# A hybrid decoder step: the sample tokens' high and low parts as 64 stationary columns, and loads of v and of the state at other places

## The chip, the cores and the metric

The kernel runs on one core of one Trainium2 chip. The metric is the device time of one execution in microseconds (us): 1620.35 us as the median of three runs, which lie between 1619.05 and 1621.43.

## The reference

One layer of a decoder, for a prompt of 1024 tokens and for 32 sample tokens (8 sequences of 4), model width 1024, everything in float32. Cut to what matters:

```python
z = x @ w_in                      # 1024 -> 4176 columns
mq, mk, mv, mo, mi, mf, aq, ak, av, iq, ik, iw = split(z)
q, k, qi, ki = partial_rope(aq), partial_rope(ak), partial_rope(iq), partial_rope(ik)
h_m, (C, n, m) = mlstm(mq, mk, mv, mo, mi, mf, C0, n0, m0)   # 4 heads of 128
idx = top_k(sum_h(iw * relu(qi @ ki)), 256)                  # the sample tokens: 65
h_a = softmax(q @ k[idx]) @ v[idx]                           # 8 heads of 64
x = layer_norm(ALPHA * x + concat(h_m, h_a) @ w_out)
y = layer_norm(ALPHA * x + (silu(x @ w_gate) * (x @ w_up)) @ w_down)
```

Outputs are y, the keys, values and indexer keys of all tokens, and the mLSTM state (C, n, m) after the prompt and after the samples. The sample tokens read their past keys and values from paged caches, and begin with a state (state_C and others) of their own.

## The kernel before, in words

**Tiles.** The tokens are nine tiles: eight of 128 prompt tokens, and a ninth (`LAST`) of the 32 sample tokens. A float32 product is made of three products of rounded parts: each operand is split into a high part (one rounding copy, on ACT) and a low part (the difference, on DVE or POOL), and PE adds high·high, high·low and low·high (`PARTS`) over 8 blocks of 128 rows (`KD`): 24 matmuls for each tile and each slice of weights.

**Projections.** The list `jobs` sets the order of the first stage on all engines. A job is one PSUM bank of a ring of six (`RING`): PE fills it and ACT or DVE empties it. Ten token-major units (iq, av, ak, aq, mv, two slices of 256 columns each, kind "tm") have the tokens as the stationary operand (L2209): 24 matmuls of 256 columns per tile, nine tiles per unit. ACT copies the bank into a row of `stage` (L2329), POOL rotates it where rope is due (`rope_tile`, L2406 to L2410), SP stores it to DRAM (`store`, L2106). After the ninth tile of most units POOL makes the low part of the weight slice two units ahead (`low`, L2418), which PE needs to begin that unit, and which needs ACT's high part (L2283). Jobs of kind "tr" (L2226) turn the rotated tiles, "scd" (L2259 on PE, copied on ACT at L2375) makes the indexer scores of the samples. Then come feature-major units mk, mq, mo (kind "fm", L2266), which ACT copies (L2382) and SP stores (L2161).

Beside this DVE selects the top-k (L2484 to L2564): it begins when the samples' scores are in SBUF, and steps through bisection passes (L2514) and the resolution of ties (L2542 to L2553). Behind it, in DVE's program, come the rows of the forget gate (`dve_rows`, b_row at L922), and ACT waits for them (`act_forget`, L959) in the middle of its copies of the "fm" jobs.

**Later stages.** Sparse attention of the prompt (`pe_attention`; L373 turns weights, L408 multiplies by v, which `sp_attention` loads at L563 from the stored output), attention of the samples (`pe_samples`, semaphore `smp_values` counts its two halves, PE L670), the mLSTM (`pe_mlstm`, nine steps n; the sample sequences use the buffer `cn`, filled from state_C, and the sample values `mvs`, both loaded in `sp_mlstm` at L892 and L894), the output product (`pe_product`, L1543, two halves h of 512 columns over nine tiles, added to x by DVE at L1613), then the FFN and the last normalisation.

**What sets the order at the mLSTM.** SP issues the loads of the prompt's and samples' values (`mv_and_one`, L620 and L623) behind the samples' cache loads, then the loads of L892 and L894, and then that of mo (L896). `pool_mlstm` waits for both halves of the samples' values and sets constants to one (L1277 to L1279). `act_columns` copies the samples' values (L1001). In step n of `act_mlstm` ACT first makes weights and keys of step n+1 (L1218, L1234), then takes the outputs of step n (`take_outputs`, L1251: four copies that are scaled by the inverse denominator of L1392), and in the later steps also makes high parts of the out weights (L1578).

## Time and profile before

| | us |
|---|---|
| median of three runs | 1620.35 |
| profiled execution: its own time | 1620.41 |
| its span on the core | 1618.6 |
| PE busy | 1566.2 (97%) |
| DVE busy | 763.0 (47%) |
| ACT busy | 449.1 (28%) |
| POOL busy | 401.9 (25%) |
| projections, about | 0 to 492 |
| prompt attention | 492 to 624 |
| samples | 625 to 654 |
| mLSTM | 656 to 730 |
| output product | 726 to 833 |
| FFN and end | 833 to 1618.6 |

The profile is of one execution, which took 0.06 us more than the median of the runs. Its span is the time between the first and the last instruction on the core, and the 1.8 us by which the execution's own time is longer lie around it. Busy time is the time in which an engine has an instruction at work; shares are of the span. The mean granted clock of PE is 0.991 of full speed.

### The profile page before, as it was taken

To read this page: it belongs to the slowest core of one execution; us is meant where nothing else is said; L and a number is where in the kernel's file an instruction comes from. 1 tells how busy PE (TensorE), PEld (TensorE's weight loads), DVE (VectorE), ACT (ScalarE), POOL (GpSimd) and SP (SyncE) were. 2 spreads that over 40 slices of the span, in tenths; PEclk is the share of its full clock that TensorE was granted. 3 is DMA by queue.
4 is the path that set the end of the run, shared out by engine and by line. 5 is a ranking of instruction groups with operands and counts; after the bars stand their busy time and mean duration, and the time that the engine had idled before them with its cause. 6 is when DMAs were issued, how large, how long until landed. Compare 5 with 4: busy or idle time off the path is not lost.

```text
span 1618.6 us, 27247 instructions
## 1 busy us (share of the span) xinstructions
PE 1566.2 (97%) x10677; PEld 1448.6 (89%) x10677; DVE 763.0 (47%) x1655; ACT 449.1 (28%) x929; POOL 401.9 (25%) x386
## 2 busy tenths in 40 slices
PE   7999999999998998689999999999999999999998
PEld 7986799999996766588789999999999999999986
DVE  2008599999834664454554413233131322413146
ACT  4336423222134564263252111211212021121100
POOL 3620155222110001425394122212221221122200
PEclk9999999999999999899999999999999999999999
DMA  5210231122216003624202111111101111111012
GB/s 183 71 43 18 64 103 49 58 85 79 80 68 253 28 21 95 182 86 160 79 1 79 53 53 53 28 53 53 53 27 53 53 49 31 53 53 53 1 53 82
DMA packets 117596, 110.65 MB, mean 68 GB/s; under 512 B 16186, under 2 KB 102206, under 8 KB 117474
## 3 DMA queue, kind: packets, MB, share of 16 engines
q1 hardware_dynamic: 117474, 108.90, 21.6%
q8 instruction: 92, 1.51, 0.4%
q14 instruction: 30, 0.25, 0.1%
HBM read 88.82 MB, written 19.95 MB: 67 GB/s over the span
## 4 chain that ended last, share of the span: by engine, by line
PE 55%; issue 0%; DVE 0%; DVEq 0%
PE bank L1765 31%; PE bank L1743 13%; PE bank L1543 6%; PE bank L1930 3%; PE bank L1925 0%; PE bank L1683 0%; PE bank L1128 0%; PE bank L1142 0%; PE bank L1145 0%; PE bank L1157 0%; DVE y_tm L1966 0%; DVE y_tm L1958 0%; DVE stats L1949 0%; DVEq L64 0%; DVE state L1353 0%
## 5 line engine op out<-in xcount | busy, mean ns | idle before, releaser
L1765 PE MATMUL bank<-x_split,gate_up_split 128*128 128x352 f32 x3168 | 510.9, 323 | 2.4 <-issue 2.4
L1765 PEld LDWEIGHTS bank<-x_split,gate_up_split 128*128 128x128 f32 x3168 | 507.5, 188 | 3.3 <-issue 3.3
L2209 PE MATMUL bank<-w_split,xT_split 128*128 128x256 f32 (+1 forms) x2160 | 271.9, 283 | 3.1 <-ACT w_split L2281 1.8
L2209 PEld LDWEIGHTS bank<-w_split,xT_split 128*128 128x128 f32 (+1 forms) x2160 | 256.8, 179 | 9.5 <-ACT kT L2365 2.9
L1848 DVE TENSOR_TENSOR hidden<-silu,bank 128x352 f32<-128x352 f32 x66 | 34.4, 522 | 411.5 <-ACT silu L1810 411.4
L1743 PE MATMUL bank<-hidden_split,weight_split 128*128 128x352 f32 x1296 | 209.2, 322 | 0.0
L1743 PEld LDWEIGHTS bank<-hidden_split,weight_split 128*128 128x128 f32 x1296 | 208.0, 188 | 0.0
L1884 POOL TENSOR_TENSOR gate_up_split<-gate_up,gate_up_split 128x2048 fp32r<-128x2048 f32 x22 | 104.3, 4741 | 376.7 <-ACT gate_up_split L1802 376.7
L2514 DVE TENSOR_SCALAR_CACHE_REDUCE chosen<-scores,level 128x384 uint8<-128x384 f32 (+2 forms) x198 | 174.3, 943 | 1.2
L1751 DVE TENSOR_TENSOR y_acc<-y_acc,bank 128x352 f32<-128x352 f32 x216 | 112.6, 521 | 84.5 <-PE bank L1743 83.3
L2266 PE MATMUL bank<-xT_split,w_split 128*128 128x352 f32 x864 | 138.8, 323 | 1.2 <-ACT feature_stage L2382 1.2
L2266 PEld LDWEIGHTS bank<-xT_split,w_split 128*128 128x128 f32 x864 | 138.3, 188 | 1.5 <-ACT feature_stage L2382 1.5
L1810 ACT ACTIVATE silu<-bank 128x352 f32<-128x352 f32 x66 | 30.7, 466 | 365.5 <-PE bank L1765 365.4
L2418 POOL TENSOR_TENSOR w_split<-w_unit,w_split 128x2048 fp32r<-128x2048 f32 (+1 forms) x16 | 73.5, 4593 | 196.7 <-ACT w_split L2283 196.7
L1543 PE MATMUL bank<-out_weight_split,x_split 128*128 128x512 f32 (+1 forms) x384 | 91.3, 396 | 0.0
L2329 ACT ACTIVATE stage<-bank 128x256 f32<-128x256 f32 (+1 forms) x90 | 34.6, 384 | 190.0 <-PE bank L2209 182.6
L1543 PEld LDWEIGHTS bank<-out_weight_split,x_split 128*128 128x128 f32 (+1 forms) x384 | 67.9, 178 | 20.4
L1888 POOL TENSOR_TENSOR weight_split<-down_weight,weight_split 128x2048 fp32r<-128x2048 f32 x10 | 46.0, 4597 | 159.5 <-ACT weight_split L1816 159.5
L1816 ACT ACTIVATE weight_split<-down_weight 128x2048 fp32r<-128x2048 f32 x10 | 19.2, 1916 | 186.6 <-PE bank L1743 186.6
L520 ACT ACTIVATE attention_weights<-attention_weights,row_minima 128x1024 f32<-128x1024 f32 (+7 forms) x64 | 49.2, 770 | 46.7 <-DVE row_minima L451 46.6
L451 DVE CUSTOM_DVE_ANT_0 attention_weights<-bank,scores 128x512 f32<-128x512 f32 (+1 forms) x48 | 30.1, 667 | 63.6 <-PE bank L362 63.6
L1802 ACT ACTIVATE gate_up_split<-gate_up 128x2048 fp32r<-128x2048 f32 x22 | 42.1, 1916 | 22.6 <-DMA gate_up<-in_w_up_dram 22.5
(293 smaller groups left out, 1641.3 us busy)
## 6 DMA issues: line engine op xcount, KB each, us to landing
w_unit<-in_w_in_dram SPq DMA_DIRECT2D x16, 1024.0 KB, 5.6
gate_up<-in_w_gate_dram SPq DMA_DIRECT2D x22, 512.0 KB, 4.0
gate_up<-in_w_up_dram SPq DMA_DIRECT2D x22, 512.0 KB, 5.3
down_weight<-in_w_down_dram SPq DMA_DIRECT2D x11, 1024.0 KB, 5.2
scratch_dram<-feature_stage SPq DMA_DIRECT2D x36, 176.0 KB, 1.8
scores<-in_x_prompt_dram SPq DMA_DIRECT2D x8, 512.0 KB, 4.9
out_dram<-stage SPq DMA_DIRECT2D x32, 128.0 KB, 1.7
out_weight<-in_w_out_dram SPq DMA_DIRECT2D x16, 256.0 KB, 6.9
```

The lines of the kernel that those rows point to most:

```text
L520: act.activation(x, x, ACT.Exp, bias=lows[:, n % 4, e, chunks[n] - 1:chunks[n]], scale=-1.0, accum_out=rowsum[:, o % 2, 2 * p + e:2 * p + ...
L1543: mm = pe.matmul(product_bank(m)[0:r, :], mix(i, a)[:, k, 0:r], wo[h][:, k, b, :], start=(k == 0 and (a, b) == PARTS[0]), stop=(k == KD - ...
L1743: mm = pe.matmul(PS[6 + n % 2][:, 0:cols.stop - cols.start], wds[:, a, k, d * P:(d + 1) * P], hs[:, 2 * s + k, b, cols], start=(k == 0 and ...
L1751: dve.tensor_tensor(y, y, PS[6 + n % 2][:, 0:cols.stop - cols.start], ALU.add).then_inc(d_added, 1)
L1765: mm = pe.matmul(PS[2 * c + w][:, 0:CH], gs[u][:, a, w, k, :], xs[:, b, k, c * CH:(c + 1) * CH], start=(k == 0 and (a, b) == PARTS[0]), st ...
L1884: pool.tensor_tensor(gs[u][:, 1], graw, gs[u][:, 0].bitcast(F32), ALU.subtract).then_inc(g_lo, 1)
L1888: pool.tensor_tensor(w[:, 1], wdraw, w[:, 0].bitcast(F32), ALU.subtract).then_inc(wd_lo, 1)
L1930: mm = pe.matmul(bank, hs[:, 2 * s + k, a, tile_cols(i)], w[:, b, k, 512 * half:512 * half + 512], start=False, stop=(s == 0 and k == 1 an ...
L2209: mm = pe.matmul(bank[0:rows(i), 0:HALF], xs1[:, a, k, tile_cols(i)], w[:, b, k, :], start=((k, a, b) == terms[0]), stop=((k, a, b) == ter ...
L2266: mm = pe.matmul(bank[:, 0:CH], wsplit[n_unit % 2][:, a, k, (m % 2) * P:(m % 2 + 1) * P], xs1[:, b, k, c * CH:(c + 1) * CH], start=(k == 0 ...
L2418: pool.tensor_tensor(lo, wraw[n >= 4][:, k], hi.bitcast(F32), ALU.subtract).then_inc(w_lo, 1)
L2514: dve.tensor_scalar(chosen[i], score[i], level_f[:, n:n + 1], 0.0, op, ALU.add, accum_out=count[:, n:n + 1]).then_inc(topk_step, 1)
```

## The change

**Sample tile.** The split of the samples' x is also written with the high and the low part side by side, as 64 stationary columns per block, for blocks 0 to 6; block 7 stays as it was. A "tm" job of the tile LAST multiplies these 64 columns by the high and by the low slice of the weights (two matmuls per block) and block 7 in three: 17 matmuls where 24 were. Rows 0 to 31 of the bank hold the high parts' sums, rows 32 to 63 those of the low parts (with low·low, which was left out before). ACT makes two copies in place of one, and POOL adds the two halves (`sum_halves`, semaphore `sample_summed`). ACT's copy of a tile LAST waits for the sum before it, its copy of "scd" for the fourth sum, and its first "fm" copy for all ten. `pe_product` does the same for its tile LAST, where DVE adds the second half with one more instruction. ACT and DVE split the samples' x (and the mixed heads) with some more instructions.

**Waits and loads.** SP's wait for all feature stores moves from the end of its first program to a place behind the nine loads of v. The loads of `cn` and `mvs` move from SP to POOL's queue, ahead of the constants of `pool_mlstm`, with a wait for the first half of the samples' values only, and for the stores of the two mv units. For steps n over 4 one DVE multiplication behind the reciprocal takes the place of ACT's four copies in `take_outputs`.

```diff
@@ sp_attention / sp_mlstm / end of SP's first program
                 sp.dma_start(v_tm[0:r, i, :], src).then_inc(v_loaded, 16)
 
+            for s in range(FST):
+                sp.wait_ge(fstored[s], 16 * (len(fm_no) // FST))
             sp_mlstm_loads(sp)
...
-            sp.wait_ge(smp_values, 1)
-            for h in range(MH):
-                sp.dma_start(mvs[SMP * h:SMP * h + SMP, 0:P], mv_dram[SEQ:T, P * h:P * h + P]).then_inc(c_in, 16)
-            for h in range(MH):
-                sp.dma_start(cn[:, h, :, 0:P], state_C[0, :, h].rearrange("b d e -> d b e")).then_inc(c_in, 16)
...
-            for s in range(FST):
-                sp.wait_ge(fstored[s], 16 * (len(fm_no) // FST))
             sp_rest(sp)
@@ act_mlstm, pool_mlstm, dve_mlstm
-                take_outputs(n)
+                if n <= MH:
+                    take_outputs(n)
...
             pool_rows_low(pool)
+            pool.wait_ge(smp_values, 1)
+            for h in range(MH):
+                pool.dma_start(cn[:, h, :, 0:P], state_C[0, :, h].rearrange("b d e -> d b e")).then_inc(c_in, 16)
+            for u in range(2):
+                s = stage_no["tm", "mv", u, LAST] % STG
+                pool.wait_ge(stored[s], 16 * seen[s])
+            for h in range(MH):
+                pool.dma_start(mvs[SMP * h:SMP * h + SMP, 0:P], mv_dram[SEQ:T, P * h:P * h + P]).then_inc(c_in, 16)
             pool.wait_ge(att_values, N2)
...
+                if n > MH:
+                    dve.wait_ge(den_done, n + 1)
+                    dve.wait_ge(h_ps, n - 1)
+                    o = o_banks[:, :, 0:2 * VE].rearrange("p b (i n) -> p b i n", n=VE)[:, :, :, 0:P]
+                    dve.tensor_tensor(htm[:, n % 2].rearrange("p (b i) n -> p b i n", b=2), o,
+                                      inv.unsqueeze(3).to_broadcast([P, 2, 2, P]), ALU.mult).then_inc(o_taken, 2)
@@ pe_product and its addition
+                if i == LAST and k < KD - 1:
+                    for b in range(2):
+                        mm = pe.matmul(product_bank(m)[0:2 * SMP, :], split_mix(k), wo[h][:, k, b, :],
+                                       start=(k == 0 and b == 0), stop=(k == 6 and b == 1))
...
+                if i == LAST:
+                    total.then_inc(sample_summed, 1)
+                    dve.wait_ge(sample_summed, len(sample_no) + h + 1)
+                    total = dve.tensor_tensor(x, product_bank(m)[r:2 * r, :], x, ALU.add)
@@ projections: PE, ACT, POOL
-                        terms = [(k, a, b) for k in range(KD) for a, b in PARTS]
+                        ks = list(range(KD)) if i < LAST else [0, 1, 2, 3, 4, 5, 7, 6]
+                        terms = [(k, a, b) for k in ks for a, b in PARTS if i < LAST or a == 0 or k == KD - 1]
...
+                            out, tokens = bank[0:rows(i), 0:HALF], xs1[:, a, k, tile_cols(i)]
+                            if i == LAST and k < KD - 1:
+                                out, tokens = bank[0:2 * SMP, 0:HALF], split_sample(k)
+                            mm = pe.matmul(out, tokens, w[:, b, k, :],
...
+                        if sample_no[job]:
+                            act.wait_ge(sample_summed, sample_no[job])
+                        act.activation(st[0:SMP, :], bank[0:SMP, 0:HALF], ACT.Copy)
+                        out = act.activation(low_of(job), bank[SMP:2 * SMP, 0:HALF], ACT.Copy)
...
                 elif kind == "scd":
+                    act.wait_ge(sample_summed, 4)
...
+            def sum_halves(job):
+
+                pool.wait_ge(freed, pos[job] + 1)
+                both = stage[0:SMP, stage_no[job] % STG, :]
+                pool.tensor_tensor(both, both, low_of(job), ALU.add).then_inc(sample_summed, 1)
...
                 if job == ("tm", "ik", 0, LAST):
+                    sum_halves(("tm", "av", 0, LAST))
...
                     low(4)
+                    sum_halves(("tm", "av", 1, LAST))
...
             for n in range(unit_no["aq", 1] + 3, len(units)):
+                if units[n - 2][0] == "mv":
+                    sum_halves(("tm",) + units[n - 2] + (LAST,))
                 low(n)
```

What the order of instructions shows of this, at three places (line numbers behind the change are those of the changed file, where L2280 is the old L2209, L2297 the old L2226, L2509 the old L2418, L2479 the new sum and L2497 to L2501 the old rope lines).

PE, the end of the second unit (iq1): its eighth and ninth tile, with the turns of the tiles before between them. Before:

```order
L2209 MATMUL bank<-w_split_73,xT_split 128x256 x24
L2226 MATMUL bank<-square,stage 128x128 x2
L2209 MATMUL bank<-w_split_73,xT_split 32x256 x24
L2226 MATMUL bank<-square,stage 128x128 x2
L2216 MATMUL bank<-xT_split,w_small_split 80x352 x24
L2226 MATMUL bank<-square,stage 128x128 x2
```

and now:

```order
L2280 MATMUL bank<-w_split_73,xT_split 128x256 x24
L2297 MATMUL bank<-square,stage 128x128 x2
L2280 MATMUL bank<-w_split_73,sample_x_split_81 64x256 x8
L2280 MATMUL bank<-w_split_73,sample_x_split_82 64x256 x4
L2280 MATMUL bank<-w_split_73,xT_split 32x256 x3
L2280 MATMUL bank<-w_split_73,sample_x_split_83 64x256 x2
L2297 MATMUL bank<-square,stage 128x128 x2
```

The ninth tile has 14 matmuls of 64 stationary columns and 3 of 32 in place of 24 of 32; the rest stands as it did.

POOL, from the last rope of the indexer's keys to the first of ak. Before (`w_split_72` is here the low part of weight slice 4, the first of ak):

```order
L2408 TENSOR_TENSOR rope_products<-stage,rope 32x2x8
L2410 TENSOR_TENSOR stage<-rope_products 32x2x16
L2435 TENSOR_SCALAR sample_index_select<-small,sample_index_weights 128x32 x2
L2418 TENSOR_TENSOR w_split_72<-w_unit_75,w_split_72 128x2048
L2406 TENSOR_TENSOR rope_products<-stage,rope 128x4x16
L2407 TENSOR_TENSOR rope_products<-stage,rope 128x4x8
L2408 TENSOR_TENSOR rope_products<-stage,rope 128x4x8
L2410 TENSOR_TENSOR stage<-rope_products 128x4x16
```

and now:

```order
L2501 TENSOR_TENSOR stage<-rope_products 32x2x16
L2479 TENSOR_TENSOR stage<-stage,sample_scores 32x256
L2527 TENSOR_SCALAR sample_index_select<-small,sample_index_weights 128x32 x2
L2509 TENSOR_TENSOR w_split_72<-w_unit_75,w_split_72 128x2048
L2479 TENSOR_TENSOR stage<-stage,sample_scores 32x256
L2497 TENSOR_TENSOR rope_products<-stage,rope 128x4x16
L2498 TENSOR_TENSOR rope_products<-stage,rope 128x4x8
L2499 TENSOR_TENSOR rope_products<-stage,rope 128x4x8
L2501 TENSOR_TENSOR stage<-rope_products 128x4x16
```

The sum of unit av0 stands ahead of `wsel` (L2435, now L2527), and that of av1 behind the low part of slice 4; `sample_scores` is the buffer that holds the low half of the sum until the samples' scores are written into it.

POOL, the beginning of its part of the mLSTM. Before:

```order
L996 TENSOR_TENSOR rows_low<-b_row,rows_high 4x1056
L996 TENSOR_TENSOR rows_low<-gates,rows_high 4x1056
L1277 MEMSET mv_and_one 128x32
L1278 MEMSET mv_by_head 128x1
L1279 MEMSET mq_by_sample 128x1152
L1284 TENSOR_TENSOR mv_by_sample_104<-mv_split,own_sample 96x8x128
L1284 TENSOR_TENSOR mv_by_sample_113<-mv_split,own_sample 96x8x128
```

and now:

```order
L1018 TENSOR_TENSOR rows_low<-b_row,rows_high 4x1056
L1018 TENSOR_TENSOR rows_low<-gates,rows_high 4x1056
L1300 DMA c_and_n_sample<-in_state_C_dram 128x8x128 x4
L1305 DMA mv_by_head<-scratch_dram 32x128 x4
L1308 MEMSET mv_and_one 128x32
L1309 MEMSET mv_by_head 128x1
L1310 MEMSET mq_by_sample 128x1152
L1315 TENSOR_TENSOR mv_by_sample_108<-mv_split,own_sample 96x8x128
```

Eight DMA issues stand now between the low parts of the rows and the three constants, and the same eight are gone from SP's queue, where they stood between the loads of `mv_and_one` and that of mo.

## Rows read from the trace of the kernel before

**Rows 1.** PE's waits by releaser, whole span (total us, times, longest us)

```profile
PE bank L1072 <- DMA c_and_n_sample<-in_state_C_dram: 3.8, 1, 3.8
PE bank L408 <- DMA v<-out_dram: 3.1, 1, 3.1
PE bank L1128 <- DVE state L1353: 2.6, 1, 2.6
...
PE bank L2266 <- ACT feature_stage L2382: 1.2, 1, 1.2
...
PE bank L2226 <- POOL stage L2410: 0.9, 2, 0.7
```

**Rows 2.** Timeline of PE, two neighbouring tiles of one unit (start, busy us)

```profile
69.55 3.08 PE L2209 MATMUL bank<-w_split,xT_split 128*128 128x256 f32 x24
...
72.60 3.06 PE L2209 MATMUL bank<-w_split,xT_split 128*32 128x256 f32 x24
```

**Rows 3.** Timeline of PE, the output product's last tile

```profile
827.03 5.79 PE L1543 MATMUL bank<-out_weight_split,x_split 128*32 128x512 f32 x24
```

**Rows 4.** Timeline of DVE, start of the top-k chain

```profile
190.14 0.18 DVE L2484 TENSOR_TENSOR sample_scores<-sample_scores,small 32x32 f32<-32x32 f32 x1 [13.97 <-ACT sample_scores L2375]
```

**Rows 5.** Timeline of POOL, low part of weight slice 4

```profile
185.34 4.57 POOL L2418 TENSOR_TENSOR w_split<-w_unit,w_split 128x2048 fp32r<-128x2048 f32 x1 [59.45 <-ACT w_split L2283]
```

**Rows 6.** Groups of POOL by line, with shapes kept apart

```profile
L1660 POOL TENSOR_TENSOR x_split<-y_acc,x_split 128x512 fp32r<-128x512 f32 x16 | 20.7, 1293 | 12.1 <-DVE x_split L1637 12.1
```

**Rows 7.** Timeline of ACT, the forget-gate rows

```profile
441.59 1.09 ACT L959 ACTIVATE m_row<-b_row 4x1056 f32<-4x1056 f32 x1 [17.96 <-DVE b_row L922]
```

**Rows 8.** Timeline of DVE, top-k's last steps

```profile
418.87 1.02 DVE L2546 SCALAR_TENSOR_TENSOR running<-running,count,equal 128x768 f32<-128x768 f32 x1
...
424.23 5.30 DVE L2546 SCALAR_TENSOR_TENSOR running<-running,count,equal 128x896 f32<-128x896 f32 x1
```

**Rows 9.** Timeline of POOL, low part of weight slice 14

```profile
423.70 4.88 POOL L2418 TENSOR_TENSOR w_split<-w_unit,w_split 128x2048 fp32r<-128x2048 f32 x1 [18.42 <-ACT w_split L2283]
```

**Rows 10.** Busy time by windows, after attention's wait (PEclk is the granted clock)

```profile
505.50:508.00 2.50, 2.50 (x32) 2.20 (x32) 0.00 (x0) 0.60 (x2) 0.00 (x0) 0.73 1.03 412
508.00:511.00 3.00, 3.00 (x20) 2.81 (x18) 1.38 (x2) 0.42 (x1) 0.00 (x0) 0.65 1.02 407
```

**Rows 11.** Timeline of SP's queue, end of the projections

```profile
492.49 0.32 SPq L2161 DMA_DIRECT2D scratch_dram<-feature_stage  x1
496.48 4.13 SPq L563 DMA_DIRECT2D v<-out_dram  x9
```

**Rows 12.** Timeline of PE, two late mLSTM steps

```profile
707.06 1.06 PE L1128 MATMUL bank<-mv_and_one,mk_weighted 128*128 128x129 f32 x8
...
711.51 1.06 PE L1128 MATMUL bank<-mv_and_one,mk_weighted 128*128 128x129 f32 x8
```

**Rows 13.** Timeline of ACT, the take of steps 6, 7 and 8

```profile
710.85 1.15 ACT L1251 ACTIVATE hidden_by_token<-bank,denominator 128x128 f32<-128x128 f32 x4 [1.16 <-DVE denominator L1392]
...
716.58 1.15 ACT L1251 ACTIVATE hidden_by_token<-bank,denominator 128x128 f32<-128x128 f32 x4 [1.16 <-DVE denominator L1392]
...
723.35 1.15 ACT L1251 ACTIVATE hidden_by_token<-bank,denominator 128x128 f32<-128x128 f32 x4 [1.16 <-DVE denominator L1392]
```

**Rows 14.** Timeline of DVE, a multiplication of the same size

```profile
723.17 0.66 DVE L1399 TENSOR_TENSOR mixT<-bank,iqT 128x512 f32<-128x512 f32 x1
```

**Rows 15.** Timeline of PE, samples' values of the first half

```profile
646.46 1.12 PE L670 MATMUL bank<-v,sample_weights_turned 32*128 32x512 f32 x2
```

**Rows 16.** Timeline of SP's queue, the state loads

```profile
655.19 7.84 SPq L894 DMA_DIRECT2D c_and_n_sample<-in_state_C_dram  x4
```

**Rows 17.** Timeline of ACT, the first use of the mLSTM sample values

```profile
656.04 0.63 ACT L1001 ACTIVATE mv_split<-mv_and_one 96x512 fp32r<-96x512 f32 x1 [3.09 <-DMA mv_and_one<-scratch_dram]
```

**Rows 18.** Timeline of POOL, the first constant of the mLSTM stage

```profile
652.44 0.15 POOL L1277 MEMSET mv_and_one<- 128x32 f32 x1 [20.77 <-PE bank L670]
```

**Rows 19.** Busy time by windows, the values' loads

```profile
650.00:655.00 5.00, 3.45 (x26) 1.36 (x19) 1.11 (x6) 0.60 (x1) 1.16 (x3) 1.00 1.08 251
```

More of the change, by code:

```diff
@@ L1532, in pe_product @@
         def pe_product(pe, h, i, between=None):
-            r, m = rows(i), h * TILES + i
+            m = h * TILES + i
             if m >= 3:
                 pe.wait_ge(added, m - 2)
-            for k in range(KD):
+            order_k = list(range(KD)) if i < LAST else [0, 1, 2, 3, 4, 5, 7, 6]
+            for k in order_k:
                 if i == 0:
@@ L1570, in mix_low @@
                 eng.wait_ge(mix_hi, 2 * i + j + 1)
-                eng.tensor_tensor(mix(i, 1)[:, k, :], mixT[:, k, tile_cols(i)], mix(i, 0)[:, k, :].bitcast(F32), ALU.subtract)\
-                    .then_inc(done, 1)
+                whole = [[(mix(i, part)[:, k, :], mixT[:, k, tile_cols(i)])] for part in range(2)]
+                for (hi, src), (lo, _) in zip(*(whole if i < LAST else [sample_mix(j, 0), sample_mix(j, 1)])):
+                    low = eng.tensor_tensor(lo, src, hi.bitcast(F32), ALU.subtract)
+                low.then_inc(done, 1)
         def out_high(act, h, j):
@@ L2319, in _ @@
                                          bank[:, :].rearrange("p (k n) -> p k n", k=4)[:, :, 0:rows(i)], ACT.Copy)
+                    for dst, src in sample_parts(j, bank, 0) if i == LAST else ():
+                        out = act.activation(dst, src, ACT.Copy)
                 elif kind == "tm":
@@ L2378, in _ @@
                     f = fm_no[job]
+                    if f == 0:
+                        act.wait_ge(sample_summed, len(sample_no))
                     if f >= FST:
```

71 lines of the change are left out of this document (58 added, 13 removed).

## Prediction

> **What bounds the kernel now.** I first read PE's waits, because PE works through nearly all of the span: the reader should see that the whole list is small, and that four entries lie where the change reaches, 3.8 us for the samples' state, 3.1 for v, 2.6 for the mLSTM state and 1.2 for ACT's feature copy, and that POOL has held PE up by 0.9 us in the first units [rows 1]. Then the timelines of PE at a sample tile, to price the matmuls. Then, because time that PE saves is only kept if nothing else sets the end of its stage, I followed ACT's longest wait in the projections back: 17.96 us until DVE's b_row, ended at 441.59 us [rows 7]. DVE works through its top-k from 190.14 us [rows 4] to there almost without a pause. So the end of the projections hangs on DVE, and PE, which runs six banks ahead, feels only 1.2 us of that wait [rows 1].
>
> A result under 0.2% (3.2 us) from 1620.35 cannot be told from no change.
>
> **A. The sample tile in the projections.** A tile with 32 stationary columns is busy for 3.06 us, one with 128 for 3.08 [rows 2]: what a matmul costs does not hang on these columns, so 64 cost the same, and one is 3.06/24 = 0.128 us. Seven fewer in each of ten units are worth 10 x 0.89 = 8.9 us of PE. I expect to collect almost none of it.
> - The first unit (iq0) loses its 0.89 to the wait for POOL (0.9 us in all) [rows 1], which hangs on the weights' loads and splits and not on PE.
> - iq1 and av0 bring everything 1.8 us forward. DVE's chain starts with the copy of the samples' scores, and that copy now waits for av1's sum, which stands on POOL behind the low part of slice 4. This part runs from 185.34 for 4.57 us [rows 5], thus ends at 189.91; moved forward by 1.8, and with the sum behind it, it ends at 188.1 + 0.65 = 188.8. The sum's 0.65 is half of the 1.29 us that POOL takes for 512 columns [rows 6]; were it 1.29, 189.4. With an estimated 0.5 us for the copy and its hand-over, DVE starts at about 189.3 in place of 190.14, 0.8 us sooner (0.2 to 0.8); av1's own 0.89 is hidden behind POOL.
> - Near its end DVE's L2546 on 896 columns took 5.30 us, where 768 columns took 1.02 [rows 8]; it started at 424.23, while POOL worked on slice 14 from 423.70 to 428.58 [rows 9], and ended with it. By the neighbour it would have taken 1.2, so 4.1 were lost. Slice 14 now comes some seven units x 0.89 = 6.2 to 7 us earlier, at about 417, and there meets the L2546 on 768 columns (418.87 before, some 418.1 now), which would then be held until 421.5: a new block of 3.4 in place of the 4.1. Between blocks of 2.6 and 4.6 us I take a gain of 0.7.
> - So DVE ends about 1.5 us sooner (0.2 to 2.3), and with it ACT's wait; PE reaches that point 7 us sooner and stands idle for about 6.7 us in place of 1.2. What follows so long a pause may run at a lower clock: after the pause of 3.1 us in attention the granted clock was 0.73 for 2.5 us and 0.65 for 3.0 [rows 10], which is 2.5 x 0.27 + 3.0 x 0.35 = 1.7 us lost. After the 1.2 us I see none. I take 1.7 (0 to 3).
>
> A is then -1.5 + 1.7, near zero: **+0.2** (-2.3 to +2.8).
>
> **B. The output product.** The row of 24 matmuls for the sample tile is busy for 5.79 us, 0.241 each [rows 3]; 14 fewer over two halves are **-3.4** us, on the path, since PE goes from this tile straight to the FFN. The second DVE addition (about 0.66 as [rows 14]) and the three more operations on the samples' mixed heads lie beside other tiles' matmuls; PE waits for POOL's and ACT's last tile only later, so I let between 2 and 3.4 through.
>
> **C. The load of v.** SP issues the last feature store at 492.49 (0.32 us long) and v only at 496.48, when its stores have landed [rows 11]: that is the 3.7 us that go. The nine issues take 4.13, PE's wait ends at 505.5, some 4.9 us after the last of them. Issued from 492.8 on, v lands at about 501.9, before PE is ready at 502.4. The 3.1 us go [rows 1], and with them the pause and the 1.7 us at a lower clock [rows 10]: **-4.8** (-2.7 if the clock falls all the same and the landing lags). What is late next is only the loads behind the moved wait, which the mLSTM needs 150 us later.
>
> **D. ACT's take.** PE's own step is 4.45 us (707.06 to 711.51) [rows 12]. ACT's takes lie 5.73 and 6.77 us apart at the end [rows 13]: take, high parts of the out weights, weights and keys fill ACT, and PE waits 2.6 us for what hangs on them [rows 1]. Without the take (1.15) ACT has no wait for the denominator in its chain either, and PE sets the step: (5.73 - 4.45) + (6.77 - 4.45) = 3.6 us. The last take falls from 1.15 to some 0.66, the time of a DVE multiplication of 128x512 [rows 14]: 0.5. DVE then has some 3.7 us of work in a 4.45 us step. **-4.1** (-2 to -4.3).
>
> **E. State and sample values.** PE waits 3.8 us, to 668.7, for the state [rows 1], which SP issues from 655.19 for 7.84 us, 1.96 each [rows 16], behind the values' loads. POOL may issue it once the first half of the samples' values is there, after PE's L670 of 646.46 [rows 15], at about 647.7. Had it nothing beside it, it would land 7 us sooner, and all 3.8 go. But from 650 to 655 the DMA engines are full (share 1.08) with the values' loads [rows 19], for which ACT waited 3.09 us until 656.04 [rows 17], and which start the stage. With half of the engines' time from 647.7 on, these loads would need up to 8.4 us more, as long as they still ran before. So E lies between -3.8 and -3.8 + 8.4 = +4.6. If POOL issues at SP's pace, the state's loads come in one by one and take less than half: I put the delay at 2.4, nearer the free end, **-1.4**. POOL's price of an issue is in no row; its constants, at 652.44 before [rows 18], are needed at about 656.
>
> The Trainium skill, in "DMA: Bandwidth & Descriptors", section "SWDGE vs HWDGE vs iDMA", says that a DMA issued from GpSimd has its descriptors computed by software, with a slower setup than one from SP, and that the two feed different queues between which each DMA engine goes round-robin. No row of this trace shows a load from POOL. By that page's fit (section "Anatomy of one DMA — SWDGE (gpsimd) path") 512 KB would take an estimated 3.2 us, which by itself would land the state in time and make the sum 1604.5; by its round-robin the values lose half, which is the second rival below.
>
> **Sum.** 0.2 - 3.4 - 4.8 - 4.1 - 1.4 = -13.5 against the profiled execution's 1620.41, which is 0.06 over the median: **1607** us.
>
> **The rivals.**
> 1. *The saved matmuls are kept.* If ACT's wait ended with PE (DVE ending over 7 us sooner), A would be -8.0 (nine units) and no clock lost: 1598.7. Against it: the 17.96 us [rows 7]. For it: 4.1 us of DVE's chain are a collision that could miss altogether [rows 8, 9]. Chance 0.12.
> 2. *State against values.* The DMA engines share evenly, E is +4.6 and the rest holds: 1613. For it: the full engines [rows 19] and ACT's wait [rows 17]; against: 7.84 us of spread issues [rows 16]. Chance 0.22.
> 3. *The pause costs more clock.* Over 3 us behind the pause of 6.7, as it is twice as long as the one in [rows 10]; A is +3: 1610. Chance 0.12.
> 4. *POOL's issues gate the mLSTM.* The constants stand behind eight issues. At SP's 1.96 us each [rows 16] they would end at 647.7 + 15.7 + 1.3 = 664.7, 8.6 late; with the state's wait gone E would be +4.8, still a gain in all (1613.2). The change becomes slower than before by 0.2% when E passes +15.3, that is when the constants are 19 us late, at 3.3 us for an issue. Then some 1624. For it: these are other issues than any in the trace, and 512-byte rows; against: four of the eight are loads of only 16 KB. Chance 0.03.
>
> **How the numbers follow.** Forecast 0.51, the rivals 0.12, 0.22, 0.12 and 0.03. The range goes from rival 1 to rival 2 with the bounds of E and D, leaving out the better part of rival 1 and of rival 4: 1600 to 1614. Faster by over 0.2%: all but rival 4 and the case that it meets rival 3, 0.94; same 0.03; slower 0.03.
>
> **What would show it.** Right: PE's list of waits without v, the state and the mLSTM state, and with 6 to 7 us at L2266 for ACT's feature copy; ACT's L959 ending at about 440; a granted clock under 1 just behind it, and 1.0 at 505; late mLSTM steps of 4.45 us; sample tiles of 17 matmuls in 2.2 us. Wrong: ACT's copy of the samples' values later than 660, POOL's constants later than 656, a DVE chain that ends where it did (then A is a loss), or PE passing the feature copies without a longer pause than before.

## The result and the profile after

The changed kernel takes 1630.28 us (median of four runs, 1629.57 to 1631.72) against 1620.89 us of the kernel before (1619.05 to 1621.54): the ratio is 1.0066, with a 95% interval of 1.005 to 1.0082. It is 9.4 us slower; 1607 had been forecast, with 1600 to 1614 as the range.

The page of the profiled execution (1630.6 us) shows at once that the matmuls did go: PE is busy for 10.4 us less than before (1566.2), and the span is 10.2 us longer (1618.6).

```profile
span 1628.8 us, 27102 instructions
...
PE 1555.8 (96%) x10593; PEld 1442.3 (89%) x10593; DVE 773.0 (47%) x1664; ACT 448.4 (28%) x927; POOL 415.2 (25%) x405
...
q0 software_dynamic: 704, 2.16, 0.5%
...
L1832 PE MATMUL bank<-x_split,gate_up_split 128*128 128x352 f32 x3168 | 515.3, 324 | 10.2 <-issue 7.8
```

The last line is the FFN's first group, which idled for 2.4 us in the kernel before and idles for 10.2 now. PE's waits by releaser (total us, times, longest us), to be held against [rows 1]:

```profile
PE bank L2337 <- ACT feature_stage L2463: 12.9, 1, 12.9
PE bank L1063 <- ACT c_and_n_sample L1031: 8.9, 1, 8.9
PE bank L1832 <- issue: 7.8, 4, 2.5
...
PE bank L1832 <- DVE hidden L1915: 2.4, 2, 1.3
```

The waits for v, for the state and for the mLSTM state are gone, as forecast. In their place stand 12.9 us for ACT's feature copies (1.2 before, 6.7 forecast), 8.9 us for a copy of ACT's at the mLSTM that was hardly waited for before, and 10.2 us in the FFN, of which the prediction said nothing.

The starts of the same PE instructions in the two timelines give the loss stage by stage (us):

| PE reaches | before | after | lead of before | change in the stage |
|---|---|---|---|---|
| the end of the pause at the feature copies | 445.56 | 451.42 | 5.86 | +5.86 |
| the first multiplication by v (L408) | 505.50 | 510.32 | 4.82 | -1.04 |
| the end of the samples' attention (L1022) | 654.51 | 657.80 | 3.29 | -1.53 |
| the mLSTM's spreads (L1041) | 657.18 | 669.00 | 11.82 | +8.53 |
| the samples' outputs (L1072) | 668.66 | 677.00 | 8.34 | -3.48 |
| a late mLSTM step (L1128) | 702.61 | 707.16 | 4.55 | -3.79 |
| the out product (L1543) | 726.29 | 727.53 | 1.24 | -3.31 |
| the FFN (L1765) | 833.45 | 831.43 | -2.02 | -3.26 |
| the end | 1618.6 | 1628.8 | 10.2 | +12.22 |

**The FFN** is the largest loss, though the change touches nothing in it. Its two groups of weights run in a loop, and PE jumps back three times. PE's timeline at the first jump, after:

```profile
1009.79 8.43 PE L1832 MATMUL bank<-x_split,gate_up_split 128*128 128x352 f32 x52
1019.47 0.74 PE L1832 MATMUL bank<-x_split,gate_up_split 128*128 128x352 f32 x3 [1.25 <-DVE hidden L1915]
1022.69 3.63 PE L1832 MATMUL bank<-x_split,gate_up_split 128*128 128x352 f32 x13 [2.47 <-issue]
```

and in the kernel before:

```profile
1017.84 2.38 PE L1765 MATMUL bank<-x_split,gate_up_split 128*128 128x352 f32 x14
1020.92 3.32 PE L1765 MATMUL bank<-x_split,gate_up_split 128*128 128x352 f32 x19 [0.70 <-issue]
```

Before, PE pauses for 0.70 us and goes on. After, it pauses for 1.25 us (put down to DVE, at the second jump to "issue"), runs three matmuls, and pauses again for 2.47, in which it waited for nothing that the profile shows. The 13 matmuls behind it are busy for 3.63 us where 19 had 3.32. At the two other jumps it is the same: the pauses sum to 10.2 us against 2.4. What is left of the 12.2 is slower matmuls behind them: PE is busy with this group for 515.3 us, before 510.9. In the 4 us behind the second pause (1022.7 to 1026.7) the granted clock was 0.61, in the same stretch of the kernel before (1020.9 to 1024.9) 1.00.

**The projections.** ACT waited 29.66 us for the row of the forget gate, which DVE gave 5.86 us later than in [rows 7]:

```profile
447.45 1.08 ACT L981 ACTIVATE m_row<-b_row 4x1056 f32<-4x1056 f32 x1 [29.66 <-DVE b_row L944]
```

DVE's chain had begun at 189.64, 0.5 us sooner than in [rows 4]. Its bisection passes began 0.5 us later all the same, here first in the kernel before and then in the changed one:

```profile
200.75 0.61 DVE L2514 TENSOR_SCALAR_CACHE_REDUCE chosen<-scores,level 128x384 uint8<-128x384 f32 x1
```

```profile
201.26 0.61 DVE L2614 TENSOR_SCALAR_CACHE_REDUCE chosen<-scores,level 128x384 uint8<-128x384 f32 x1
```

The eight rounds ahead of the passes, whose code is the same, took 1.0 us longer, with short idle times in each of them that the kernel before does not have. The first of these:

```profile
191.18 0.44 DVE L2603 MATCH_REPLACE8 sample_scores<-eight_largest,sample_scores 32x288 f32<-32x288 f32 x1 [0.32 <-issue]
```

From the chain's start to the first pass it is 11.6 us in the changed kernel and in every run with an edit of it, and 10.6 in the kernel before; why, no run shows.

What made the chain much longer is seen in one of its passes, here with DVE's two short operations between passes, and below with POOL at the same time:

```profile
246.49 4.15 DVE L2625 TENSOR_SCALAR flip<-count 128x6 int32<-128x6 f32 x1
250.67 0.17 DVE L2628 SCALAR_TENSOR_TENSOR level<-flip,level 128x6 int32<-128x6 int32 x1
```

```profile
245.32 4.59 POOL L2509 TENSOR_TENSOR w_split<-w_unit,w_split 128x2048 fp32r<-128x2048 f32 x1
249.88 0.31 POOL L2497 TENSOR_TENSOR rope_products<-stage,rope 128x64 f32<-128x64 f32 x1
...
250.37 0.24 POOL L2499 TENSOR_TENSOR rope_products<-stage,rope 128x32 f32<-128x32 f32 x1
```

The row of flips (128x6) takes 0.17 us when nothing is in its way. Here it took 4.15: it came while POOL made the low part of a weight slice, and was held past the end of that through three rope operations which follow without a gap. Of the ten low parts that POOL made beside the chain, five held DVE up by over 2 us in the kernel before (14.0 us for four of them in the passes, 4.1 for the one of [rows 8]) and a sixth by 0.6; now eight did (20.3 for seven in the passes, 4.3 for one in a later step). All short operations together (busy us, mean ns), first before, then after:

```profile
L2525 DVE TENSOR_SCALAR flip<-count 128x6 int32<-128x6 f32 x32 | 16.1, 502 | 1.1
L2528 DVE SCALAR_TENSOR_TENSOR level<-flip,level 128x6 int32<-128x6 int32 x32 | 10.3, 322 | 1.1
```

```profile
L2625 DVE TENSOR_SCALAR flip<-count 128x6 int32<-128x6 f32 x32 | 26.0, 814 | 1.1
L2628 DVE SCALAR_TENSOR_TENSOR level<-flip,level 128x6 int32<-128x6 int32 x32 | 5.7, 178 | 1.1
```

That is 5.3 us more. With 0.1 for the later step and the 1.0 of the rounds, less the 0.5 of the sooner start, it makes the 5.86 to 0.1 us.

What follows the pause runs at about half clock, near the lower of the two levels (1.2 GHz of 2.4). The columns are the busy us of PE, PEld, DVE, ACT and POOL, then PEclk, the granted clock; 4.00 x (1 - 0.53) = 1.9 us are lost in the first of these windows:

```profile
452.00:456.00 4.00, 4.00 (x16) 4.00 (x15) 3.97 (x3) 3.98 (x6) 1.04 (x1) 0.53 0.77 270
456.00:460.00 4.00, 4.00 (x27) 4.00 (x26) 4.00 (x2) 0.65 (x2) 4.00 (x1) 1.00 0.12 45
```

**The mLSTM.** ACT's first use of the samples' values, in place of 656.04 and 3.09 in [rows 17]:

```profile
667.86 0.63 ACT L1023 ACTIVATE mv_split<-mv_and_one 96x512 fp32r<-96x512 f32 x1 [11.62 <-DMA mv_and_one<-scratch_dram]
```

POOL had issued the state from 651.19 and the samples' values behind it:

```profile
651.19 3.75 POOL L1300 DMA_DIRECT2D c_and_n_sample<-in_state_C_dram  x4 [16.16 <-PE bank L697]
654.93 2.02 POOL L1305 DMA_DIRECT2D mv_by_head<-scratch_dram  x4
656.92 0.18 POOL L1308 MEMSET mv_and_one<- 128x32 f32 x1
```

POOL's issues of 512 KB took 0.94 us each, those of 16 KB 0.5, and its constants came at 656.92, before PE's wait began. It is the transfers that were late (KB each, median us from issue to landing):

```profile
mv_and_one<-scratch_dram SPq DMA_DIRECT2D x8, 256.0 KB, 4.8
c_and_n_sample<-in_state_C_dram POOLq DMA_DIRECT2D x4, 512.0 KB, 9.3
...
mv_and_one<-scratch_dram SPq DMA_DIRECT2D x3, 64.0 KB, 11.8
```

The three small loads that ACT waits for took 11.8 us to land, where they had taken 4.2.

**The late mLSTM steps and the product** are as forecast: every step is 4.45 us, as in [rows 12],

```profile
707.16 1.06 PE L1150 MATMUL bank<-mv_and_one,mk_weighted 128*128 128x129 f32 x8
...
711.61 1.06 PE L1150 MATMUL bank<-mv_and_one,mk_weighted 128*128 128x129 f32 x8
...
716.05 1.06 PE L1150 MATMUL bank<-mv_and_one,mk_weighted 128*128 128x129 f32 x8
...
720.50 1.06 PE L1150 MATMUL bank<-mv_and_one,mk_weighted 128*128 128x129 f32 x8
```

and the sample tile of the product takes 17 matmuls, 4.00 us from its start to that of the next instructions at 830.64, where the tile of [rows 3] took 5.63:

```profile
826.64 3.01 PE L1597 MATMUL bank<-out_weight_split,sample_mix 128*64 128x512 f32 x12
829.49 0.84 PE L1601 MATMUL bank<-out_weight_split,x_split 128*32 128x512 f32 x3
830.17 0.64 PE L1597 MATMUL bank<-out_weight_split,sample_mix 128*64 128x512 f32 x2
```

### The profile page after: what moved, and what is told of

It reads as the page before. It is cut to its first block, busy times and chain, and to the rows that moved or that the text cites. A ratio compares the mean times of both kernels' runs of the same rounds, so it can differ in the third digit from the quotient of the medians.

```text
span 1628.8 us, 27102 instructions
## 1 busy us (share of the span) xinstructions
PE 1555.8 (96%) x10593; PEld 1442.3 (89%) x10593; DVE 773.0 (47%) x1664; ACT 448.4 (28%) x927; POOL 415.2 (25%) x405
## 3 DMA queue, kind: packets, MB, share of 16 engines
q8 instruction: 91, 1.49, 0.4%
## 4 chain that ended last, share of the span: by engine, by line
PE 57%; issue 1%; POOL 0%; DVE 0%; ACT 0%; DVEq 0%
PE bank L1832 31%; PE bank L1810 13%; PE bank L1601 6%; PE bank L1997 3%; PE bank L1992 0%; PE bank L1750 0%; PE bank L1164 0%; PE bank L1597 0%; PE bank L1167 0%; POOL c_and_n_sample L1319 0%; PE bank L1150 0%; PE bank L1130 0%; PE bank L1100 0%; PE bank L1179 0%; POOL mv_by_sample L1315 0%
## 5 line engine op out<-in xcount | busy, mean ns | idle before, releaser
L1832 PE MATMUL bank<-x_split,gate_up_split 128*128 128x352 f32 x3168 | 515.3, 324 | 10.2 <-issue 7.8
L2280 PE MATMUL bank<-w_split,xT_split 128*128 128x256 f32 (+1 forms) x1950 | 247.7, 284 | 3.8 <-POOL w_split L2509 2.0
L2280 PEld LDWEIGHTS bank<-w_split,xT_split 128*128 128x128 f32 (+1 forms) x1950 | 234.3, 187 | 8.4 <-issue 3.8
L2337 PE MATMUL bank<-xT_split,w_split 128*128 128x352 f32 x864 | 140.6, 326 | 12.9 <-ACT feature_stage L2463 12.9
L2509 POOL TENSOR_TENSOR w_split<-w_unit,w_split 128x2048 fp32r<-128x2048 f32 (+1 forms) x16 | 73.5, 4593 | 162.7 <-ACT w_split L2354 162.7
L1601 PE MATMUL bank<-out_weight_split,x_split 128*128 128x512 f32 (+1 forms) x342 | 81.6, 396 | 0.0
L1601 PEld LDWEIGHTS bank<-out_weight_split,x_split 128*128 128x128 f32 (+1 forms) x342 | 63.4, 186 | 15.5
L2402 ACT ACTIVATE stage<-bank 128x256 f32<-128x256 f32 x80 | 30.7, 384 | 161.2 <-PE bank L2280 150.7
```

What stands on the lines that cost most here:

```text
L1601: mm = pe.matmul(product_bank(m)[0:rows(i), :], mix(i, a)[:, k, :], wo[h][:, k, b, :], start=(k == 0 and (a, b) == PARTS[0]), stop=(i < LA ...
L1832: mm = pe.matmul(PS[2 * c + w][:, 0:CH], gs[u][:, a, w, k, :], xs[:, b, k, c * CH:(c + 1) * CH], start=(k == 0 and (a, b) == PARTS[0]), st ...
L2280: mm = pe.matmul(out, tokens, w[:, b, k, :], start=((k, a, b) == terms[0]), stop=((k, a, b) == terms[-1]))
L2337: mm = pe.matmul(bank[:, 0:CH], wsplit[n_unit % 2][:, a, k, (m % 2) * P:(m % 2 + 1) * P], xs1[:, b, k, c * CH:(c + 1) * CH], start=(k == 0 ...
L2509: pool.tensor_tensor(lo, wraw[n >= 4][:, k], hi.bitcast(F32), ALU.subtract).then_inc(w_lo, 1)
```

## Experiments

**Where PE's code lies.** The theory: 84 matmuls, each a weight load and a matmul, are 168 instructions fewer ahead of the FFN's loop. They move the loop's head within the blocks in which PE's code is fetched.

```diff
+        code_pad = sem("code_pad")
...
+            for _pad in range(16):
+                pe.sem_inc(code_pad, 1)
             pe.wait_ge(square_in, 16)
```

> The changed kernel with 16 increments of an unused semaphore ahead of PE's first instruction, where PE waits for x anyway; nothing else. Theory of code placement: the 84 matmuls fewer (168 instructions) have moved the head of the FFN loop to the last few instructions of a 16 KB block of PE's code, so that after each of the three jumps back PE runs 3 matmuls and waits 2.2 to 2.5 us for the next block. 16 instructions more put the head at the start of a block: the second pause goes, the FFN takes some 785 us as before in place of 797, and the time is about 1618 to 1620. Rival, the FFN is slower by late data or by the clock: no change, 1630.

Measured: 1622.35 us (ten runs, 1619.1 to 1626.32), ratio to before 1.0016 (1.0001 to 1.0031). The FFN takes 785.1 us, to the tenth what it took before. PE at the first jump:

```profile
1017.77 2.71 PE L1833 MATMUL bank<-x_split,gate_up_split 128*128 128x352 f32 x16
1021.17 3.01 PE L1833 MATMUL bank<-x_split,gate_up_split 128*128 128x352 f32 x17 [0.70 <-issue]
```

The total came 2 us higher than expected: the mLSTM's wait was 11.0 us in this run, where the changed kernel had 8.9. The reverse, the same lines with 88 increments in the kernel before:

> The kernel before with 88 increments of an unused semaphore ahead of PE's first instruction; nothing else. 88 more and 168 fewer instructions put the loop's head at the same place of a 256-instruction block. Theory of code placement: the FFN gets the same second pauses of over 2 us at three places, 785 becomes about 797 us, and the time is about 1631 to 1633. Rival: no change, 1621.

Measured: 1637.51 us, ratio 1.0096 (1.007 to 1.0123). The FFN takes 797.6 us, with the same picture of three matmuls and a second pause:

```profile
1026.82 0.74 PE L1766 MATMUL bank<-x_split,gate_up_split 128*128 128x352 f32 x3 [1.12 <-DVE hidden L1849]
1029.89 4.57 PE L1766 MATMUL bank<-x_split,gate_up_split 128*128 128x352 f32 x19 [2.33 <-issue]
```

The rest above the expected time is that 88 increments held PE up at its start (it waited 14.4 us where it waits 5.9). Both directions are shown: the 12.2 us in the FFN come from where the loop lies in PE's code, and from nothing else in the change. That what counts is how far its head stands from the end of a block is a reading of this. In the Trainium skill, "Runtime: NRT & Kernel Launch", section "Instruction fetch mechanics", code comes in blocks of 16 KB, 256 instructions, and a jump to a place that is not held has to wait for its block. The runs agree: the page counts 91 transfers and 1.49 MB on one instruction queue, 16.4 KB each, there is a pause at each jump, and a second one after three matmuls goes and comes with a few instructions ahead of the loop. In the changed kernel one of these transfers lies inside the second pause, between 1019.8 and 1021.2:

```profile
q8 instruction: 1, 0.02, 5.6%
```

In the kernel before, the transfer that follows the jump lies between 1021.3 and 1022.4, while PE runs its 19 matmuls.

**Whether DVE's loss is a matter of phase.** In a model with POOL's times from the trace, a pass of 5.73 us, and a short operation held to the end of a low part, DVE's last pass ends by estimate at 405.1 for the kernel before (405.0 in the trace) and at 411.0 for the changed one (410.8). POOL's times of the changed kernel alone, or alone the 0.5 us by which its passes begin later, give the same whole pass more in the model. The model also says that any delay of 0.5 to 7.5 us costs one whole pass in the kernel before, and no more:

```diff
+            for _late in range(24):
+                dve.sem_inc(code_pad, 1)
             dve.memset(level, 0).then_inc(topk_step, 1)
```

> The kernel before with 24 increments of an unused semaphore on DVE ahead of the top-k passes, which then begin some 1 us later; nothing else. Theory of locked phase: of DVE's 33 passes (5.73 us each) one whose short operations start while POOL makes the low part of a weight slice (4.6 us) is held until that ends; a model with the trace's POOL times gives the same end for starts up to 5 us sooner and one pass more (5.9 us) for a start 0.5 us later. So DVE's row of the forget gate ends at about 447.5 in place of 441.6, PE's pause there becomes about 7 us with up to 2 us of lower clock behind it: about 1627 to 1629. Rival, the delay just adds to DVE's chain: DVE ends 1 us later and the time is 1622.

Measured: DVE's first pass began at 203.32 us, where it had been 200.75. The delay was thus 2.6 us, more than meant, and the row came here:

```profile
446.33 1.24 DVE L923 SCALAR_TENSOR_TENSOR b_row<-gates 4x1056 f32<-4x1056 f32 x1
```

In the kernel before it had started at 440.31. It is 6.0 us later and not 2.6, PE's pause at the feature copies 6.9 us, 1627.57 us (ratio 1.0027, 1.0003 to 1.0051). Seven of ten runs lay between 1626 and 1630 and three between 1615 and 1621. That the chain ended a pass sooner in those three, by which side of a low part it fell on, is a reading: the one trace of this kernel is of a run of the seven.

**Shorter blocks.** POOL's low part in eight operations of 256 columns:

```diff
-                pool.tensor_tensor(lo, wraw[n >= 4][:, k], hi.bitcast(F32), ALU.subtract).then_inc(w_lo, 1)
+                raw = wraw[n >= 4][:, k]
+                for c in range(hi.shape[1]):
+                    piece = pool.tensor_tensor(lo[:, c], raw[:, c], hi[:, c].bitcast(F32), ALU.subtract)
+                piece.then_inc(w_lo, 1)
```

> The changed kernel where POOL makes the low part of a weight slice in 8 operations of 256 columns in place of one of 2048; nothing else. Theory that POOL holds up DVE: a DVE operation is now held for one small operation (some 0.7 us) at most, so the 24.6 us that eight blocked operations cost fall to a few; DVE's row of the forget gate ends before PE gets there (about 425 to 432), PE's pause of 12.9 us at the feature copies and the half clock behind it go, and the time falls by some 13 to 15 us, to about 1616. Rival, DVE's chain is longer for a reason of its own: the pause stays, 1630; or PE then waits for POOL, whose low parts take 5.5 to 6 us in place of 4.6.

Measured: 1631.11 us, no gain; the expectation failed. The eight operations take 5.6 us, DVE's chain began 5 us later (PE waited 6.9 us for POOL's rope), and DVE was still held through many of POOL's operations in a row:

```profile
255.13 4.65 DVE L2628 TENSOR_SCALAR flip<-count 128x6 int32<-128x6 f32 x1
```

and later:

```profile
336.53 0.64 DVE L2628 TENSOR_SCALAR flip<-count 128x6 int32<-128x6 f32 x1
337.20 0.65 DVE L2631 SCALAR_TENSOR_TENSOR level<-flip,level 128x6 int32<-128x6 int32 x1
```

In the second place each of the short operations waited for one of POOL's, as expected, in the first for a whole row of them. What decides between the two was not found.

**Out of the way.** DVE's flips in PSUM, so that neither short operation has both its data in SBUF; on top of the 16 increments:

```diff
         PS = [psum[:, 512 * i:512 * i + 512] for i in range(8)]
+        flip = PS[6].bitcast(I32)[:, 0:n_sparse]
```

> The changed kernel with the 16 increments ahead of PE's program (the kernel a_pad16), and one buffer moved: DVE's row of flips between two top-k passes lies in PSUM in place of SBUF, so that neither of the two short operations has both its data in SBUF. Theory that these two operations are what POOL's low parts hold up: none of them takes over 0.5 us any more, the 20 us of blocks go but for one in the last steps, DVE's row of the forget gate ends at about 425 to 430 in place of 447, PE's pause at the feature copies (13 us) and the half clock behind it go, and the time falls by 13 to 15 us to about 1606 to 1608. Rival, the block does not depend on where the data lies: 1621.

Measured: 1604.88 us, ratio 0.9925 (0.9902 to 0.9948). At the same place, under the same low part (245.45 to 250.05), nothing is held:

```profile
246.98 0.17 DVE L2629 TENSOR_SCALAR bank<-count 128x6 int32<-128x6 f32 x1
247.18 0.16 DVE L2632 SCALAR_TENSOR_TENSOR level<-bank,level 128x6 int32<-128x6 int32 x1
```

ACT's wait for DVE ends at 430.8, PE gets through without a pause:

```profile
430.80 1.08 ACT L983 ACTIVATE m_row<-b_row 4x1056 f32<-4x1056 f32 x1 [12.87 <-DVE b_row L946]
```

Against the kernel a_pad16, measured at another time, that is 17.5 us by the medians and some 15 by the two ratios; the first multiplication by v starts at 495.5 in place of 511.3. This agrees with the Trainium skill's "SBUF — State Buffer", section "Who interferes with whom": DVE and GpSimd share a port pair as an exclusive lock, which DVE needs for a second input from SBUF or for a 2-port performance mode. Which of the two held which of the short operations, no run shows. The section has the lock held for one whole instruction; the flip of 4.15 us above was held 0.7 us beyond the end of the low part, and there the measurement decides. The same line in the kernel before:

> The kernel before with the flips in PSUM; nothing else. Theory: in the kernel before, DVE's blocks (18 us) cost only the 1.2 us that PE waited, since PE had no time saved; DVE's row ends at about 425 to 430, and the time is 1 to 2 us less, about 1618 to 1619. If the before kernel gains 5 us or more, what p_flip gained is not the changed kernel's saved matmuls.

Measured: 1617.47 us, ratio 0.9987 (0.9976 to 0.9998). DVE's row starts at 425.29, 15 us sooner, and the kernel gains under 3 us by it: the blocks were there all the time, and cost little as long as PE was not ahead of them.

**The state's loads.** Back on SP, as before the change, on top of a_pad16:

```diff
@@ pool_mlstm
-            for h in range(MH):
-                pool.dma_start(cn[:, h, :, 0:P], state_C[0, :, h].rearrange("b d e -> d b e")).then_inc(c_in, 16)
...
@@ sp_mlstm
+            sp.wait_ge(smp_values, 1)
...
+            for h in range(MH):
+                sp.dma_start(cn[:, h, :, 0:P], state_C[0, :, h].rearrange("b d e -> d b e")).then_inc(c_in, 16)
             sp.wait_ge(rows_split, 16 * 9)
```

> The kernel a_pad16 with the loads of the state and of the samples' values back on SP's queue, where they stood before; all other parts of the change stay. Theory that the state's loads crowd out the values' loads: ACT's first use of the samples' values waits some 3 us in place of 11.6, PE's wait of 9 to 11 us for it goes, and PE waits 2 to 4 us for the state instead; from the end of the samples' part to the fourth step of the mLSTM the stage is 1 to 3 us shorter. Rival, the delay comes from POOL's own issue of the loads or from elsewhere: the wait stays.

Measured: 1617.21 us, ratio 0.9991 (0.9976 to 1.0005). ACT waited 2.73 us for the samples' values, PE 2.3 for the state:

```profile
661.87 0.63 ACT L1029 ACTIVATE mv_split<-mv_and_one 96x512 fp32r<-96x512 f32 x1 [2.73 <-DMA mv_and_one<-scratch_dram]
```

```profile
PE bank L1100 <- DMA c_and_n_sample<-in_state_C_dram: 2.3, 1, 2.3
```

From the samples' end to the out product it is 63.2 us, against 71.8 in a_pad16 and 71.8 before the change. The other way, the samples' values first:

```diff
+            for part in range(3):
+                sp.dma_start(mv3[SMP * part:SMP * part + SMP], mv_dram[SEQ:T, :].rearrange("t (h n) -> t h n", h=MH))\
+                    .then_inc(mv3_loaded, 16)
             for i in range(LAST):
                 sp.dma_start(mvx[:, i, :, 0:P],
...
-            act.wait_ge(mv_loaded, 16 * (LAST + 3))
+            act.wait_ge(mv3_loaded, 16 * 3)
```

> The kernel a_pad16 with the three small loads of the samples' values (64 KB each) ahead of the eight of the prompt's values on SP's queue, with a semaphore of their own. Theory that it is the sharing of the DMA engines between state and values, and the small loads' place behind the large ones: ACT's first use comes at its time (about 3.3 us after the samples' part), PE's wait for it goes (9 to 11 us), and all loads are in by the time of the samples' outputs, or PE waits there for the prompt's values for up to 4 us; 5 to 9 us less, about 1613 to 1616. Rival: the small loads are late wherever they stand, no change.

Measured: 1616.05 us, ratio 0.9978 (0.9964 to 0.9992). ACT's wait is gone, the small loads land in 2.7 us, and the prompt's values, now beside the state, land in 10.1 where they took 4.8; PE waits for those:

```profile
PE bank L1095 <- DMA mv_and_one<-scratch_dram: 2.9, 1, 2.9
```

Both edits take PE's wait of 9 to 11 us away; other waits, of 2.3 and 2.9 us, come in its place, and by the medians the runs are 5.1 and 6.3 us under a_pad16. POOL's issue was not slow; the state's loads took the DMA engines from the loads that were wanted first.

**Together.** First the flips and the order of the values' loads, then the flips and the state's loads on SP, both with the 16 increments:

> The kernel a_pad16 with both edits of p_flip and p_mv3. If both theories hold the gains add: some 20 us under a_pad16, about 1599 to 1602, clearly under the kernel before. If only one holds, its gain alone.

Measured: 1602.9 us, ratio 0.9904 (0.9887 to 0.9921), a little above the 1599 to 1602 expected.

> The changed kernel with the three edits that each gave time alone: 16 increments ahead of PE's program, the flips in PSUM, and the loads of the state and of the samples' values back on SP's queue. If the three losses are separate, the sum of the stages of p_flip and p_sp holds: 642.9 us to the end of the samples, 63.2 to the out product, 104 for it, 785 for the FFN, about 1597. If the state's loads on SP meet other transfers now that the stages before are shorter: up to 1604.

Measured: 1603.22 us, ratio 0.99 (0.9876 to 0.9923), not 1597. Both beat both kernels, but the loads' edit adds little to p_flip that can be told. In the profile of p_best DVE began 3.0 us later than in p_flip, behind weights that landed later, and PE's granted clock in the middle of the mLSTM was lower (from 680 to 690 us 0.84, in p_flip 1.00). Whether these two go with the edit or with the run stays open.

**The takes.** p_best with ACT's four copies in all steps:

```diff
-                if n <= MH:
-                    take_outputs(n)
+                take_outputs(n)
...
-                if n > MH:
...
-                    dve.tensor_tensor(htm[:, n % 2].rearrange("p (b i) n -> p b i n", b=2), o,
-                                      inv.unsqueeze(3).to_broadcast([P, 2, 2, P]), ALU.mult).then_inc(o_taken, 2)
```

> The kernel p_best with the outputs of the late mLSTM steps taken by ACT again, as before. Theory of the prediction (ACT's chain sets the late steps): the last steps take 5.7 and 6.8 us in place of 4.45, 3 to 4 us more than p_best. Rival, another wait takes the place: under 1 us.

Measured: 1607.21 us, 4.0 more than p_best. ACT's last takes are again 5.71 and 6.76 us apart, as in [rows 13], and PE's last three steps take 15.55 us in place of 12.34:

```profile
699.47 1.14 ACT L1280 ACTIVATE hidden_by_token<-bank,denominator 128x128 f32<-128x128 f32 x4 [1.17 <-DVE denominator L1421]
...
705.18 1.14 ACT L1280 ACTIVATE hidden_by_token<-bank,denominator 128x128 f32<-128x128 f32 x4 [1.17 <-DVE denominator L1421]
...
711.94 1.14 ACT L1280 ACTIVATE hidden_by_token<-bank,denominator 128x128 f32<-128x128 f32 x4 [1.17 <-DVE denominator L1421]
```

**Without the 64 columns.** The kernel before with the flips in PSUM, the moved wait and the takes on DVE:

> The kernel before with the flips in PSUM, the wait for the feature stores behind the loads of v, and the late takes on DVE: the change without the 64 columns and without the loads on POOL. Against b_flip 4.4 us for v with the clock behind it and 3.3 for the takes: about 1611. p_best should lie under it by the matmuls saved, 70 in the projections less those of the first unit (8) and 14 in the out product (3.3): 11 us. If it lies under it by 4 us or less, the 64 columns are not what p_best gains by.

Measured: 1609.52 us, ratio 0.9939 (0.9916 to 0.9963). The wait and the takes are worth 8.0 us against b_flip, 7.7 had been expected. p_best lies 6.3 us under b_cd, p_flip, with the loads on POOL and measured at another time, 4.6: the columns are worth something, but less than the 11 us expected. Of the 6.3 us 3.3 are the out product, which takes 107.2 us in b_cd and 103.9 in p_best.

## Why the prediction was wrong

**A, the projections, forecast +0.2 (-2.3 to +2.8), measured +7.8.** What was right: the saved matmuls are not collected, the end hangs on DVE, the chain starts sooner by under a microsecond (0.5; forecast 0.8), slice 14 comes at about 417 (417.87) and meets another operation for about the same price (4.3 us for 4.1), and PE stands idle with a lower clock behind it (1.9 us; forecast 1.7). The step that failed is "Between blocks of 2.6 and 4.6 us I take a gain of 0.7", from which "DVE ends about 1.5 us sooner" follows. It moved one block of 4.1 us and took the rest of DVE's chain as fixed. Four more blocks, 14.0 us in all, stood in the passes before it, and their number depends on POOL's timing against the 5.73 us of a pass. POOL's low parts now came 1.6 us sooner at the first pass (205.06 for 206.64) and 5.8 at slice 14, the passes began 0.5 us later, and seven blocks were there in place of four. In the trace of the kernel before, an operation of 128x6 that takes 0.17 us stands with 4.53; the prediction names no such row.

**B, the product, forecast -3.4, measured -3.26. C, v, forecast -4.8, measured -4.4**: 2.95 for the wait and 1.42 behind it for the clock (the table's rows hold this with the 1.9 us lost behind the pause). **D, the takes, forecast -4.1, measured -3.3**, and 4.0 in the run that undid it. These three held by their own steps.

**E, the state, forecast -1.4 (-3.8 to +4.6), measured +1.26** from the samples' end to the step at 702.61. Up to the samples' outputs it is +5.05 (8.53 and -3.48 in the table). Behind them the stage is 3.79 us shorter, with a granted clock of 0.83 before (669.2 to 702.6) and of 0.92, then 1.00 after (677.6 to 707.2), which no step of the prediction names: luck. The step that failed is "I put the delay at 2.4, nearer the free end". The delay was 8.5, the "up to 8.4 us more" from which rival 2 took its +4.6. Rival 2 named the mechanism and the row, but the sum leaned to the free end because of SP's spread issues; POOL issued twice as fast (0.94 us against the 1.96 of [rows 16]). A load of 512 KB took 9.3 us to land beside the values' loads, where 3.2 had been estimated for one by itself.

**The FFN, not in the sum, measured +12.22.** No step of the prediction is about it; the sum took for granted that a stage whose code is unchanged takes the same time. This alone turns the result: without it this execution would have ended 2.0 us under the kernel before, which cannot be told from no change, and a_pad16, in which it is gone, measured 0.16% above. Rival 4, the slow one, named another place: POOL's constants came in time.

The sum: -13.5 forecast; A 7.6 more, B 0.1, C 0.4, D 0.8, E 2.7 and the FFN 12.2 give +10.3, measured +10.2.

## What to carry to other kernels

When code ahead of a loop grows or shrinks, look at PE's pauses at the jump back before and after: a few instructions of padding ahead of the loop can be worth as much as the matmuls that were saved. When PE's savings run into another engine, price that engine's whole chain, with every operation that takes many times its usual length, since the length of such a chain depends on what the others do beside it. And a load that is moved forward takes its bytes from the loads that are in flight there: order them by who is waited for first.

## What was not expected of the hardware

- A jump back on PE costs 0.70 to 1.00 us here, or 3.1 to 3.7 us and slower matmuls behind it at a granted clock of 0.61, by where the loop lies in PE's code; 16 instructions moved that by 12.3 us over three jumps.
- A delay of 2.6 us at the start of DVE's chain came out as 6.0 us at its end. The model's reading: operations that run into POOL's are held to POOL's end and so fall into step with it.
- DVE was held not only through one POOL operation but through several that followed each other without a gap (4.15 us under a low part of 4.59 that ended 0.7 us sooner, and 4.65 us beside eight operations of 0.7). Of the seven flips held in the changed kernel five were let go with the end of the low part, two 0.7 us later.
- An operation of 128x6 with its output in PSUM ran in 0.17 us under the same POOL operation that held it for 4.15 with its output in SBUF.
